# A two-block transformer on one core: the columns of two stationary weight tiles alternate in memory

## What is computed

```python
def swiglu(h, w_in, w_out):
    gate, up = jnp.split(h @ w_in, 2, axis=-1)
    return (jax.nn.silu(gate) * up) @ w_out

def half_ffn(h, m, k, g_pre, g_post, w_in, w_out):
    y = swiglu(modulated_norm(h, g_pre, m, k), w_in, w_out)
    return gated_residual(h, y, g_post, m, k, 0.5)
```

## Time and profile before

| | us |
|---|---|
| median of 3 executions | 2420.63 (2419.8 to 2421.6) |
| profiled execution, first to last instruction (span) | 2419.5 |
| PE busy (matmuls) | 2384.9 |
| PEld busy (weight loads, beside the matmuls) | 2059.6 |
| DVE busy | 1600.1 |
| ACT busy | 1063.2 |

### The profile page before, as it was taken

The page is one execution under the profiler, slowest core; times in us unless marked ns, Lnnn a source line. Parts: engine busy times, 40 slices in busy tenths (PEclk is TensorE's granted clock), DMA queues, the critical chain, the costliest instruction groups (busy, mean ns, idle before and its releaser), DMA issues.

```text
span 2419.5 us, 36353 instructions
## 1 busy us (share of the span) xinstructions
PE 2384.9 (99%) x14712; PEld 2059.6 (85%) x14712; DVE 1600.1 (66%) x2899; ACT 1063.2 (44%) x1882; POOL 0.2 (0%) x4
## 2 busy tenths in 40 slices
PE   9999999999999999999999999999999999999998
PEld 5888888976788888888888888899998998999997
DVE  7776775477587677377623357655586776877767
ACT  4222324455552223252223245644556556555663
POOL 0000000000000000000000000000000000000000
PEclk9999999999999999999999999999999999999999
DMA  6554552211125455215522212245534443444432
GB/s 275 207 195 188 202 198 70 88 53 53 71 91 197 186 198 203 87 55 207 207 107 90 102 70 88 111 157 181 191 142 157 175 140 127 167 169 158 157 123 88
DMA packets 48408, 346.53 MB, mean 143 GB/s; under 512 B 5361, under 2 KB 5489, under 8 KB 6769
## 3 DMA queue, kind: packets, MB, share of 16 engines
q1 hardware_dynamic: 48242, 344.21, 38.3%
HBM read 343.14 MB, written 1.05 MB: 142 GB/s over the span
## 4 chain that ended last, share of the span: by engine, by line
PE 92%; DVE 5%; ACT 2%; issue 1%; DMA 0%; SPq 0%; DVEq 0%; ACTq 0%
PE ps L484 26%; PE ps L485 25%; PE ps L486 25%; PE ps L826 1%; PE ps L828 1%; PE ps L827 1%; DVE w_lo L2119 1%; PE ps L873 1%; PE ps L1030 1%; PE ps L654 1%; ACT w_hi L1430 1%; PE ps L679 1%; PE ps L1056 1%; PE ps L859 1%; PE ps L608 1%
## 5 line engine op out<-in xcount | busy, mean ns | idle before, releaser
L1430 ACT ACTIVATE w_hi<-ring 128x1024 fp32r<-128x1024 f32 x494 | 523.4, 1060 | 1052.5 <-PE ps L486 988.9
L2119 DVE TENSOR_TENSOR w_lo<-ring,w_hi 128x1024 fp32r<-128x1024 f32 x494 | 603.5, 1223 | 422.8 <-ACT w_hi L1430 419.5
L484 PE MATMUL ps<-u_hi,w_hi 128*128 128x512 f32 (+1 forms) x1856 | 656.8, 354 | 4.8 <-DVE u_lo L2192 2.3
L485 PE MATMUL ps<-u_lo,w_hi 128*128 128x512 f32 (+1 forms) x1856 | 648.6, 349 | 0.0
L486 PE MATMUL ps<-u_hi,w_lo 128*128 128x512 f32 (+1 forms) x1856 | 648.4, 349 | 0.0
L484 PEld LDWEIGHTS ps<-u_hi,w_hi 128*128 128x128 f32 x1856 | 348.4, 188 | 60.9 <-issue 7.7
L485 PEld LDWEIGHTS ps<-u_lo,w_hi 128*128 128x128 f32 x1856 | 348.5, 188 | 47.3 <-issue 0.5
L486 PEld LDWEIGHTS ps<-u_hi,w_lo 128*128 128x128 f32 x1856 | 348.6, 188 | 45.5
L484 PE MATMUL ps<-uh,w_hi 128*128 128x256 f32 x1136 | 321.9, 283 | 2.9 <-DVE w_lo L2119 1.7
L2107 DVE CUSTOM_DVE_ANT_0 waste<-ring,condb,cols 128x1024 f32<-128x1024 f32 x260 | 322.3, 1279 | 0.1
L486 PE MATMUL ps<-uh,w_lo 128*128 128x256 f32 x1136 | 315.4, 278 | 0.0
(11 more groups left out here) (364 smaller groups left out, 2686.6 us busy)
## 6 DMA issues: line engine op xcount, KB each, us to landing
ring<-in_wk SPq DMA_DIRECT2D x317, 1024.0 KB, 4.8
mix<-in_wk SPq DMA_DIRECT2D x3, 1024.0 KB, 16.2
yT<-in_wk SPq DMA_DIRECT2D x2, 1024.0 KB, 7.8
hT<-in_x SPq DMA_DIRECT2D x1, 2048.0 KB, 13.1
htabs<-in_htabs SPq DMA_DIRECT2D x1, 1088.0 KB, 7.3
out_t<-uT SPq DMA_DIRECT2D x2, 512.0 KB, 2.6
trig<-in_trig SPq DMA_DIRECT2D x3, 256.0 KB, 7.5
wuk<-in_uk SPq DMA_DIRECT2D x2, 256.0 KB, 5.1
```

The source lines that it names most:

```text
L484: mm(bank, hi, x_hi, start=first, stop=False, skip_group_check=skip)
L485: mm(bank, hi, x_lo, start=False, stop=False, skip_group_check=skip)
L1430: f(half_hi(K, 0, HALF), ringed(n, K % 2 * HALF, (K % 2 + 1) * HALF), ACT.Copy).then_inc(whi_ready, 1)
L2119: tt(half_lo(K, 0, HALF), ringed(HALF_SLOT[K], K % 2 * HALF, (K % 2 + 1) * HALF), half_hi(K, 0, HALF).bitcast(F32), ALU.subtract).then_inc ...
```

## The change

The host packs the columns of each pair of 128-column tiles alternately: column 0 of the even tile, column 0 of the odd tile, column 1 of the even tile, and so on, 256 columns for a pair. Slots of 2P-wide tiles (the value projections and the first adaptive-normalisation slots) and those packed by `rows` stay as they were. In the kernel two new helpers, `tile_hi` and `tile_lo`, give tile `k` of a half as a pattern of 128 columns with a step of two elements (8 bytes), beginning at column 0 or 1 of its pair. They replace `half_hi` and `half_lo` in all nine places where weights are the stationary operand, in `column`, `half_column`, `two_columns`, `first_columns`, `chunk`, and the blocks of the mixers and the second stage. Transfers, the splitting into high and low parts, and the moving operands are written as before. On every engine the sequence of instructions is that of before; only line numbers in the file move. The diff, with three of its parts (the other call sites are changed in the way of the second):

```diff
--- before.py
+++ after.py
@@ -371,6 +371,14 @@
             n = (h % NW) * HALF
             return w_lo[:, n + a:n + b]
 
+        def tile_hi(h, k):
+            n = (h % NW) * HALF + k // 2 * 2 * P + k % 2
+            return w_hi[:, n:n + 2 * P - 1:2]
+
+        def tile_lo(h, k):
+            n = (h % NW) * HALF + k // 2 * 2 * P + k % 2
+            return w_lo[:, n:n + 2 * P - 1:2]
+
         def tile(buf, k, a=0, n=S):
             return buf[:, k * S + a:k * S + a + n]
 
@@ -516,7 +524,7 @@
                     if ready is not None:
                         pe.wait_ge(ready, seen - (KC - 1 - k) * per)
                     at_k = slice(k * stride, k * stride + T)
-                    last = three(bank[:, 0:T], half_hi(H, k * P, (k + 1) * P), half_lo(H, k * P, (k + 1) * P),
+                    last = three(bank[:, 0:T], tile_hi(H, k), tile_lo(H, k),
                                  xh[:, at_k], xl[:, at_k], k == 0, k == KC - 1)
                 last.then_inc(half_done, 1)
                 H += 1
...
@@ -724,8 +732,8 @@
 
                 def chunk(j, m, c0=0, c1=T):
                     h = (hids + j) % NH * TT
-                    return three(ps[OUT_BANK[m]][:, c0:c1], half_hi(H + j, m * P, (m + 1) * P),
-                                 half_lo(H + j, m * P, (m + 1) * P), h_hi[:, h + c0:h + c1], h_lo[:, h + c0:h + c1],
+                    return three(ps[OUT_BANK[m]][:, c0:c1], tile_hi(H + j, m),
+                                 tile_lo(H + j, m), h_hi[:, h + c0:h + c1], h_lo[:, h + c0:h + c1],
                                  j == 0, j == FT - 1 or parted and j == FT - NW - 1, parted and j >= FT - NW)
 
                 for j in range(FT - NW):
...
@@ -2945,6 +2953,9 @@
             k, width = w.shape[0] // P, c1 - c0
             to = self.a[self.n, :, at:at + k * width].reshape(P, k, width)
             to[...] = w[:, c0:c1].reshape(k, P, width).transpose(1, 0, 2)
+            if width != 2 * P:
+                to = self.a[self.n, :, at:at + k * width].reshape(P, -1, P, 2)
+                to[...] = to.reshape(P, -1, 2, P).transpose(0, 1, 3, 2).copy()
             at += k * width
         self.n += 1
 
```

More of the change, by code:

```diff
@@ L581, in two_columns @@
                     for b in range(2):
-                        last = three(banks[b][:, 0:T], half_hi(H + b, k * P, (k + 1) * P),
-                                     half_lo(H + b, k * P, (k + 1) * P), xh[:, at_k], xl[:, at_k], k == 0, k == KC - 1)
+                        last = three(banks[b][:, 0:T], tile_hi(H + b, k),
+                                     tile_lo(H + b, k), xh[:, at_k], xl[:, at_k], k == 0, k == KC - 1)
                         if k == KC - 1:
@@ L632, in block @@
                     at_k = slice(k * TT + s * S, k * TT + (s + 1) * S)
-                    return three(bank[:, s * S:(s + 1) * S], half_hi(h, k * P, (k + 1) * P),
-                                 half_lo(h, k * P, (k + 1) * P), u_hi[:, at_k], u_lo[:, at_k], k == 0, k == KC - 1)
+                    return three(bank[:, s * S:(s + 1) * S], tile_hi(h, k),
+                                 tile_lo(h, k), u_hi[:, at_k], u_lo[:, at_k], k == 0, k == KC - 1)
                 def side_by_side(s):
@@ L910, in block @@
                 def block(b, k):
-                    last = three(banks[b][:, :], half_hi(H + b, k * P, (k + 1) * P),
-                                 half_lo(H + b, k * P, (k + 1) * P), u_hi[:, k * TT:(k + 1) * TT],
+                    last = three(banks[b][:, :], tile_hi(H + b, k),
+                                 tile_lo(H + b, k), u_hi[:, k * TT:(k + 1) * TT],
                                  u_lo[:, k * TT:(k + 1) * TT], k == 0, k == KC - 1)
@@ L964, in project_out @@
                             at_k = slice(k * TT + s * S, k * TT + (s + 1) * S)
-                            last = three(banks[i][:, s * S:(s + 1) * S], half_hi(H + i, k * P, (k + 1) * P),
-                                         half_lo(H + i, k * P, (k + 1) * P), u_hi[:, at_k], u_lo[:, at_k],
+                            last = three(banks[i][:, s * S:(s + 1) * S], tile_hi(H + i, k),
+                                         tile_lo(H + i, k), u_hi[:, at_k], u_lo[:, at_k],
                                          k == 0, k == KC - 1)
@@ L1167, in _ @@
                         for b in range(2):
-                            last = three(pair[b][:, 0:S], half_hi(H + b, k * P, (k + 1) * P),
-                                         half_lo(H + b, k * P, (k + 1) * P), tile(lead_hi, k), tile(lead_lo, k),
+                            last = three(pair[b][:, 0:S], tile_hi(H + b, k),
+                                         tile_lo(H + b, k), tile(lead_hi, k), tile(lead_lo, k),
                                          k == 0, k == KC - 1)
@@ L1387, in _ @@
                             for k in range(4):
-                                last = three(bank, half_hi(H, (t * 4 + k) * P, (t * 4 + k + 1) * P),
-                                             half_lo(H, (t * 4 + k) * P, (t * 4 + k + 1) * P),
+                                last = three(bank, tile_hi(H, t * 4 + k),
+                                             tile_lo(H, t * 4 + k),
                                              tile(br_hi[p], k), tile(br_lo, BR_AT[p] + k), k == 0, k == 3)
```

## The result

The changed kernel takes 2466.25 us (median of 4 runs, 2465.87 to 2467.81), the kernel before 2420.22 us on the same chip. The ratio is 1.0195, 95% interval 1.0181 to 1.021: slower by 46 us. The forecast was no change, 2420.6 us. The time lies inside the range (2360 to 2490), 4 us from what rival 1 gave (2470), but the sign was missed.

A forecast was written before the change was run, and what follows sets the result against it. The prediction took PE's load-and-matmul steps as the bound. All terms were 0, so 2419.5 + 0 = 2419.5 us for the profiled execution, forecast as a median of 2420.6 us, range 2360 to 2490 us.

The forecast's parts named there:

- rival 1: Strided loads held to the widest read's rate: 7 ns per narrow (256-column) step, 50 us, 2470 us; 0.18 with weak form.
- What bounds the kernel: PE, busy 2384.9 of 2419.5 us: the time is the number of load-and-matmul steps times the length of a step.
- Instructions, transfers, splitting at 0: Unchanged instruction sequences, same-size transfers and elementwise hi/lo splitting on ACT and DVE: cost 0 each.
- The load at 0 ns: 11928 weight loads reading every second fp32 element keep their time, adding 0 ns; chance of unchanged load 0.37.
- Wide steps hidden: 512-column steps, 4824 of them, stay at 229 ns, with 124 ns left over the load's 105 ns.
- Rival 2: Load takes twice as long per column: narrow steps 116.3 to 218 ns, 725 us more, 3145 us; chance 0.09.
- Rival 3: Stride takes load and stream reads out of each other's way: narrow steps all at quick pace, 21 us gained, 2400; chance 0.36.

The follow-up runs named there:

- The table: Step tables without the model: 128-column weight loads beside streams of varied width, stride and start; 128x128 steps took 111.7 ns at step 1, 117.8 at step 2.
- the third table: Step table without the model, 36 steps each, varying moving width and the starts of stationary and moving tiles; 512 columns at step 2 took 233.3 ns.

## Why the prediction was wrong

**What bounds the kernel**: right. PE's steps were the whole time, DMA, ACT and DVE stayed out of it, and the counts of 4824, 7104 and 864 steps are those over which the loss spreads. **Instructions, transfers, splitting at 0**: right; packing alone gives 0.9999, and ACT and DVE have the same durations as in the earlier trace rows.

**The load at 0 ns**: this step failed. With a step of two it takes 6 ns more (111.7 to 117.8 where it sets the step), and the term that I put at 0 us measured 27 us in the narrow steps. I chose the end given by the transposes' loads, 9.2 bytes per ns, on the ground that a loader which covers memory at nearly the 9.8 needed in one kind of load will do so in another. The strided load covers 1024 bytes in 117.8 ns, 8.7 bytes per ns, and "nearly" was the whole difference. The load's own slack was the better argument: I had counted 9 to 13 ns left in a narrow step and noted that part of it may be a fixed turn-round. The table shows that it is. Where the load alone sets the step it takes 111.7 ns, not 105, so the quick pace of 113.3 ns had under 2 ns to spare and the slow one 6. At 117.8 ns per load the quick pace is impossible, and nearly all narrow steps settle at 120.0 ns. Why at 120.0 and not at 117.8 is open; the table has 120.0 at 256 columns for contiguous tiles too, at relative start 0. Rival 1 had this mechanism and its sign: a load held to 8.9 bytes per ns, 115 ns. But it set the 115 ns against 105 and not against 111.7, and took 7 ns per narrow step where 3.7 were measured (50 us for 27), and it left the wide steps unchanged.

**Wide steps hidden**: this failed too. That the 2470 us of rival 1 lie near the result is luck: its narrow term was twice too large, and the wide term that it had at nothing made up for it. I had written that a change in the wide steps would prove that the load's reads act on the stream. Something of the load does reach the stream, and it needs no longer load: 4.3 ns (21 us) come with the stride, and about the same with contiguous loads that begin 4 bytes off. The step of a stream depends on the width and on where the two reads start. That the two reads get in each other's way is the likely reading; how they do it is not shown.

**Rival 2**: right that it needs a step of four. There the Trainium skill's rule (Advanced Engine Details and Errata, SBUF Cachelines; two hits on a 16-byte line are needed) points the right way: 118 ns at two elements and 233 at four (128 moving columns), 175 at three (256 moving columns). Its "full performance" is not met to the end, as 112 became 118, and a stream with a step of two in its moving operand, also two hits per line, took twice as long (226.7 to 453.3 ns). **Rival 3**: wrong in sign. Its observation (two paces with the same instructions) may come from the same effect as the 21 us of the wide steps, but no run shows that. The rule of the Trainium skill set against it (TensorE: Matmul & The Clock Gate, Step-by-step: what each phase is for; two independent read ports, nothing taken from the running matmul) does not fit these fp32r streams: a wide step goes from 226.7 to 233.3 ns when only the start of the weight tile moves.

**Chances**: I gave rivals 1 and 2 together 0.27 because I took the nearest row for a proof that the load would keep its rate. A load path at its limit in seven thousand steps deserved more: with so little slack, any slowing shows, while nothing in the trace showed a way to gain.

## What to carry to other kernels

Where a weight load and its matmul take nearly the same time (here 112 and 113 ns at 256 fp32r columns), the load pattern is on the path: keep stationary tiles contiguous, and avoid four fp32 elements of step, which doubled the load here. To estimate a strided load, count the 16-byte pieces it touches, at some 1.8 ns each, and take 112 ns as the least for 128 columns. Measure the shortest load-bound step (128 moving columns) before calling anything slack; a record's slope per column misses the turn-round. Judge a change of pattern by the starts of the wide steps as well, since "the load ends long before" does not protect them. And compare single terms over several runs before crediting a few us to a change: the paces of narrow steps shift by themselves.

## What was not expected of the hardware

- An fp32r stream of 512 columns with contiguous operands never ran at 213 ns (one column per cycle at 2.4 GHz) in the tables, but at 226.7 ns at best, 17/16 of it. With only 32 or 64 stationary columns loaded beside it, it was slower still (231.7 and 230.1).
- The starts of stationary and moving tile move 128x512 between 226.7 and 237.2 ns and 128x256 between 113.3 and 126.7 ns in the third table, with contiguous tiles throughout. At 512 columns an odd first element is as bad as a stride.
- Strided stationary reads: 111.7, 117.8 and 233.5 ns per load at steps of 1, 2 and 4 fp32 elements; 175 at 3 and 241 at 8 in 256-column steps. Strided moving reads: twice the time already at a step of 2.
- Why the reads fall into these rhythms, and what selects 113.3 or 117.7 ns at one relative start, stays open.
